# Adaptive sums moved from TensorE to VectorE, and the first taps of a depthwise convolution moved from VectorE to TensorE

## The reference, cut to what matters

```
silu_c = jax.nn.silu(c)
silu_cc = jax.nn.silu(c_ctx)
for i in range(DEPTH):
    mod_x = (silu_c @ ada_w[i] + ada_b[i])[:, None, :]
    mod_c = (silu_cc @ ada_w[i] + ada_b[i])[None, None, :]
    sx1, cx1, gx1, sx2, cx2, gx2 = jnp.split(mod_x, 6, axis=-1)
    sc1, cc1, gc1, sc2, cc2, gc2 = jnp.split(mod_c, 6, axis=-1)
```

```
z = h @ pw1_w + pw1_b
a, g = jnp.split(z, 2, axis=-1)
u = a * jax.nn.sigmoid(g)
u = dwconv(u, dw_w, dw_b)              # 31 taps, each channel by itself
u = jax.nn.silu(layernorm(u, ln_g, ln_b))
return u @ pw2_w + pw2_b
```

## Time and profile before

| | us |
|---|---|
| median of 3 runs | 1666.97 (1666.66 to 1667.65) |
| the profiled execution, its own time | 1666.32 |
| its span in the trace | 1664.5 |
| TensorE, matmuls busy | 1645.6 (99%) |
| VectorE busy | 956.1 (57%) |
| ScalarE busy | 675.9 (41%) |
| GpSimd busy | 174.3 (10%) |
| mean granted TensorE clock | 0.998 of full speed |

### The profile page before, as it was taken

How to read it: one execution, slowest core, us unless ns; L and a number is a source line. 1 busy time by engine, 2 the same in 40 slices (tenths; PEclk the granted TensorE clock), 3 DMA queues, 4 the chain that set the end, 5 groups by cost and what they waited for, 6 DMA issues and landing times.

```text
span 1664.5 us, 25807 instructions
## 1 busy us (share of the span) xinstructions
PE 1645.6 (99%) x10126; PEld 1437.0 (86%) x10126; DVE 956.1 (57%) x1498; ACT 675.9 (41%) x1015; POOL 174.3 (10%) x190
## 2 busy tenths in 40 slices
PE   8999989999999999999999999999999999999998
PEld 6777758998888888888899999999999888888888
DVE  6999987753433332234358665756566754543445
ACT  4656667632323222223354433324145533332334
POOL 1488841000000000000000000000000000000001
PEclk9999999999999999999999999999999999999999
DMA  9666642121222112212113120212112223232321
GB/s 384 233 236 246 252 190 79 62 86 38 73 70 72 54 63 65 67 59 69 45 52 94 63 76 33 83 51 70 57 59 78 97 88 117 89 100 89 101 88 52
DMA packets 40729, 165.74 MB, mean 100 GB/s; under 512 B 5089, under 2 KB 6369, under 8 KB 34497
## 3 DMA queue, kind: packets, MB, share of 16 engines
q1 hardware_dynamic: 38384, 151.55, 26.5%
q0 software_dynamic: 2256, 12.98, 2.2%
HBM read 162.41 MB, written 2.10 MB: 99 GB/s over the span
## 4 chain that ended last, share of the span: by engine, by line
PE 78%; DVE 5%; ACT 2%; issue 0%; DVEq 0%; ACTq 0%
PE ps L663 78%; DVE rstd L1637 1%; DVE H_lo L1672 1%; DVE w_lo L1631 1%; DVE tmp L1660 1%; DVE sq L1660 0%; DVE rstd L1648 0%; ACT sq L1230 0%; DVE X L1995 0%; ACT tmp L1230 0%; ACT H_hi L1221 0%; DVE H_lo L1670 0%; ACT tmp L1358 0%; DVE conv L2108 0%; PE ps L1076 0%
## 5 line engine op out<-in xcount | busy, mean ns | idle before, releaser
L663 PE MATMUL ps<-H_hi,w_hi 128*128 128x512 f32 (+1 forms) x1712 | 582.9, 340 | 4.0 <-DVE H_lo L1670 2.7
L663 PE MATMUL ps<-H_lo,w_hi 128*128 128x512 f32 (+1 forms) x1712 | 578.4, 338 | 0.0
L663 PE MATMUL ps<-H_hi,w_lo 128*128 128x512 f32 (+1 forms) x1712 | 577.9, 338 | 0.0
L663 PEld LDWEIGHTS ps<-H_hi,w_hi 128*128 128x128 f32 x1712 | 324.6, 190 | 57.2 <-issue 19.1
L663 PEld LDWEIGHTS ps<-H_hi,w_lo 128*128 128x128 f32 x1712 | 324.5, 190 | 35.1
L663 PEld LDWEIGHTS ps<-H_lo,w_hi 128*128 128x128 f32 x1712 | 324.8, 190 | 34.4
L1631 DVE TENSOR_TENSOR w_lo<-w_raw,w_hi 128x1024 fp32r<-128x1024 f32 x208 | 255.2, 1239 | 107.8 <-ACT w_hi L1183 74.8
L663 PE MATMUL ps<-mid_hi,w_hi 128*128 128x512 f32 (+1 forms) x592 | 199.4, 337 | 0.5
L663 PE MATMUL ps<-mid_lo,w_hi 128*128 128x512 f32 (+1 forms) x592 | 198.1, 335 | 0.0
L663 PE MATMUL ps<-mid_hi,w_lo 128*128 128x512 f32 (+1 forms) x592 | 198.1, 335 | 0.0
L2139 DVE SCALAR_TENSOR_TENSOR tmp<-ps,par,tmp 128x511 f32<-128x511 f32 x66 | 41.6, 657 | 231.3 <-ACT tmp L1516 155.0
(11 more groups left out here) (277 smaller groups left out, 2109.6 us busy)
## 6 DMA issues: line engine op xcount, KB each, us to landing
w_raw<-in_w_units SPq DMA_DIRECT2D x190, 512.0 KB, 3.5
ada<-in_ada_groups SPq DMA_DIRECT2D x38, 1024.0 KB, 6.4
w_raw<-in_w_units SPq DMA_DIRECT2D x16, 384.0 KB, 3.3
ada<-in_ada_groups POOLq DMA_DIRECT2D x4, 1024.0 KB, 10.5
ada_more<-in_ada_groups POOLq DMA_DIRECT2D x4, 1024.0 KB, 13.3
X<-in_x_cols SPq DMA_DIRECT2D x4, 768.0 KB, 7.5
w_raw<-in_w_units POOLq DMA_DIRECT2D x2, 512.0 KB, 14.2
ada_half<-in_ada_groups POOLq DMA_DIRECT2D x1, 1024.0 KB, 19.3
```

Source lines behind the costliest of these rows:

```text
L663: return nc.tensor.matmul(o, a, b, start=first, stop=last, skip_group_check=True)
```

## The change

Two things are changed.

**1. The second layer's adaptive sums leave TensorE.** The 12 groups of layer 1 are no longer loaded, multiplied or transposed. Layer 0 keeps its 12. Instead, the matrix of layer 1 comes transposed as 48 tiles of 128 output channels x 1024 inputs (`ada_cols`). After the norm ahead of the first FFN, GpSimd loads SiLU's two input vectors, spread to all partitions (`c_rows`), and then these tiles, 512 KB each, into two buffers (`mod_tile`). In the first FFN VectorE multiplies a tile with the vector and sums along the row in one instruction: 64 jobs, 32 for the 16 tiles that both streams need and 32 for the latents alone. They stand behind each pair from the second on, three in a slot and four in the last. A buffer is loaded again once its job is done (`mod_job`). VectorE's loop over the pairs is written out. Before the last output phase both ScalarE and VectorE wait until layer 1's modulation is made (`mod_ready`, 16).

**2. Two or four of the sum taps go to TensorE.** In blocks 0, 2, 4, 6 the first two sum taps, in blocks 1, 3, 5 the first four are matmuls with diagonal matrices (`first_sums`), amid the gate unit of the next block, after its second or third of eight input tiles. ScalarE makes the diagonals (`sum_diagonals`), and adds the bias to the sum in PSUM; VectorE goes on from there. Both weight splits of a block move to its start on ScalarE and VectorE.

```
+PE_SUM = [2, 4]
+MOD_TILES = 48
+MOD_BUFS = 2
+MOD_JOBS = [(j, v) for j in range(2 * KT) for v in range(2)] + [(j, 0) for j in range(2 * KT, MOD_TILES)]
+MOD_SLOTS = FT - 1
...
@ gpsimd
+            pool.wait_ge(h_lo_ready, KT * PARTS_BEFORE[3])
+            for v in range(2):
+                pool.dma_start(silu_rows[v], c_rows[v:v + 1, :].to_broadcast([P, D])).then_inc(c_rows_in, 16)
+            for n, (j, _) in enumerate(MOD_JOBS):
+                if n >= MOD_BUFS:
+                    pool.wait_ge(mod_job, n - MOD_BUFS + 1)
+                pool.dma_start(mod_tile[:, n % MOD_BUFS, :], ada_cols[j]).then_inc(mod_tile_in[n % MOD_BUFS], 16)
...
@ tensor
+            def first_sums(n, made, b):
+
+                pe.wait_ge(sum_diag_ready, made)
+                pe.wait_ge(both_ready, b + 1)
+                for j in range(n):
+                    m = mm(sum_acc, sum_diag[:, j, :], both_phases[:, j:j + HALF], j == 0, j == n - 1)
+                m.then_inc(sum_seeded, 1)
...
+                    pe.wait_ge(sig_ready, b)
+                    streams = [(slot(0, 1), LATS), (ps[:, 5, 0:CTX], CTXS)]
+                    unit, steps = 4 * i + 2 * q, 2 if q else 3
+                    unit_product(unit, 2 * q, KT, (H_hi, H_lo), streams, None, None, 0, steps)
+                    first_sums(PE_SUM[1 - q], 6 * i + (2 if q else 0), 2 * i + (q - 1))
+                    unit_product(unit, 2 * q, KT, (H_hi, H_lo), streams, k0=steps)
+                    pe.wait_ge(slot_read[0], b + S_PW1 // 2)
+                    unit_product(unit + 1, 2 * q + 1, KT, (H_hi, H_lo),
+                                 [(slot(0, 0), LATS), (ps[:, 2, 0:CTX], CTXS)], first_done=value_lat_done)
+                    if q:
+                        ada_transposes(i + 4)
+                    else:
+                        ada_products(i + 4)
...
@ scalar
+                split_hi(2 * b + 4, (2 * b + 4) % RING)
+                split_hi(2 * b + 5, (2 * b + 5) % RING)
                 act.wait_ge(slot_read[0], S_PW1 // 2 + b + 1)
                 if b >= 2:
                     act.wait_ge(conv_ready, b - 1)
-                products(b, range(0, 6))
-                ada_copy(2 * b + 5)
-                split_hi(2 * b + 4, (2 * b + 4) % RING)
-                products(b, range(6, 11))
+                products(b, range(0, 4))
+                if b and b % 2 == 0:
+                    ada_copy(b // 2 + 4)
...
+                if b < KT - 1:
+                    act.wait_ge(sum_seeded, b + 1)
+                    A(sum_acc, sum_acc, ACT.Identity, bias=sum_w[:, ODD_TAPS * KT + b:ODD_TAPS * KT + b + 1]) \
+                        .then_inc(sum_biased, 1)
+                products(b, range(4, 11))
...
@ vector, the loop over blocks
-                taps(b, range(0, LEAD))
-                ada_sum(4 + 2 * b, 0, 4 + b)
-                taps(b, range(LEAD, 6))
-                split_lo(2 * b + 4, (2 * b + 4) % RING)
...
+                for u in (2 * b + 4, 2 * b + 5):
+                    split_lo(u, u % RING)
+                even_tap(b, 0)
+                if b % 2:
+                    ada_sum((b - 1) // 2 + 4, 0, (b - 1) // 2 + 4)
+                even_tap(b, 1)
+                n = PE_SUM[b % 2]
+                for j in range(n, EVEN_TAPS):
+                    sum_tap(b, j)
+                    if j - n + 2 < DVE_EVEN:
+                        even_tap(b, j - n + 2)
...
@ vector, the first FFN, behind each pair
+            def mod_jobs(slot):
+
+                for n in range(len(MOD_JOBS) * (slot - 1) // MOD_SLOTS, len(MOD_JOBS) * slot // MOD_SLOTS):
+                    j, c = MOD_JOBS[n]
+                    buf = mod_tile[:, n % MOD_BUFS, :]
+                    dve.wait_ge(silu_rows_ready, 2)
+                    dve.wait_ge(mod_tile_in[n % MOD_BUFS], 16 * (n // MOD_BUFS + 1))
+                    v.tensor_tensor_reduce(buf, buf, silu_rows[c], 1.0, 0.0, ALU.mult, ALU.add,
+                                           accum_out=mod[:, 1, j, c:c + 1]).then_inc(mod_job, 1)
...
+                        modulation(len(MOD_JOBS), 1, 0, 48, 13)
+                        dve.wait_ge(mod_ready, 16)
                         out_phase_norm(blk, s, x_at, both, 3 + 2 * layer)
```

215 lines of the change are left out of this document (113 added, 102 removed).

## The result

| | before | changed |
|---|---|---|
| median (lowest to highest), us | 1667.31 (1666.66 to 1668.09), 4 runs | 1676.29 (1673.48 to 1679.12), 4 runs |
| ratio to before, 95% interval | | 1.0054 [1.0036, 1.0071] |
| mean granted TensorE clock of the runs | 0.998 in the profiled one | 0.995, 0.994, 0.993, 0.992 from the fastest to the slowest |
| profiled execution, its span | 1666.32, 1664.5 | 1673.48, 1671.7 |

The account below looks back on a forecast made before the run. VectorE, slower than TensorE by half a microsecond, was taken to bound the convolution loop, TensorE the whole; -9.9 us in the loop and +2.0 in the last slot gave -7.9, 1659.1 us, range 1654 to 1667.

Parts of the forecast that it names:

- loop, blocks 0 to 7: Convolution loop: VectorE saves 12.0 us and gives back 2.1, so 9.9 us shorter, 20.6 us a block.
- norm and second pointwise product: Stage behind the loop: TensorE's part is hidden behind ScalarE and VectorE; taken as 0, between -0.5 and +0.5 us.
- first FFN's pairs and three output phases: First FFN: VectorE's slot with jobs takes 15.5 us against 16.61 for a pair, so 20 slots cost nothing.
- last slot: End of first FFN: the output phase waits for the last four jobs and modulation; 2.0 us, between 0 and 5.
- VectorE's saving in the loop: Blocks 1 to 6: fewer sum taps and reductions, 1.52 us in even and 2.47 in odd blocks, together 12.0 us.
- the price of the block's start: Loop: VectorE's two splits at the block's start partly meet GpSimd's adds; 0.35 us more a block, 2.1 over six.
- The pair: VectorE's two weight splits at a block's start: 0.7 us less to 0.9 us more than now, 0.35 more taken.
- That GpSimd has 21.29 us of work: Rival, loop: GpSimd becomes the bound at 21.29 us a block, gaining only 5.9 us; 1663 us, chance 0.18.
- They start when the convolution's last row is made and move as a whole: The 49.14 us of norm and second pointwise product behind the loop, on chains through ScalarE and VectorE, keep their length.
- the jobs: First FFN: 64 VectorE jobs of 1.22 us each fit in the slots; pairs stay 16.6 us apart.
- the hand-over: Loop: VectorE's wait for TensorE's seeded sum and ScalarE's bias costs nothing, 1.4 us of cover; the rival's chance 0.17.
- "DVE blocks DMA" trap: First FFN: if jobs delayed GpSimd's loads by 1.2 us, a slot of 16.7 us, still covered; 1660 to 1661 us.

Follow-up runs that it names:

- e4: The change with four sum taps on TensorE in every block, where it has two in the even ones; 1672.61 us, 1.0035.
- e9: e7 with one even tap moved to VectorE from the ScalarE product and GpSimd add, leaving GpSimd 14 adds; 1668.34 us, 1.0005.
- e5: The change with the ninth adaptive group's products moved ahead of TensorE's wait for the last block's values; 1673.44 us, 1.0032.
- e1: The change with short matmuls added in TensorE's waits, 10 before seeded sums of two taps and 30 before the layer norm's mean; 1677.41 us, 1.0057.
- e10: e7 with 14 short matmuls on TensorE ahead of the tenth group's products, during its wait for the last row; 1668.25 us, 1.0002.
- e13: The change with 2 of GpSimd's 64 loads in the first FFN, jobs multiplying the two silu(c) rows with each other; 1674.00 us, 1.0049.
- e7: The change with four sum taps every block, ninth group's products earlier, jobs ending a slot earlier, last adaptive group's load ahead of a weight load; 1669.07 us, 1.0009.
- e14: The change with all 64 loads but VectorE's jobs of 32 columns in place of 1024; 1674.05 us, 1.0054.
- e3: The change with VectorE's two splits of a block put back behind sum taps 6 and 13; 1689.38 us, 1.0128.

## Why the prediction was wrong

The forecast was 1659.1 us, the range 1654 to 1667, with 0.11 for slower. In the profiled executions the terms are, forecast and measured:

| term | forecast | measured |
|---|---|---|
| loop, blocks 0 to 7 | -9.9 | -3.6 |
| last block, up to the first variance | 0 | +3.3 |
| norm and second pointwise product | 0 | +0.1 |
| first FFN's pairs and three output phases | 0 | +1.65 |
| last slot | +2.0 | +1.9 |
| end of the span | 0 | +2.7 |
| start to block 0 | 0 | +1.2 |

They add up to +7.2 us, from 1664.5 to 1671.7. The profiled run is the fastest of the four; the slowest has a span of 1677.3 and a clock of 0.992 for 0.995. A mean clock lower by 0.003 over 1677 us is 5 us of TensorE's full pace withheld, about the 5.6 us by which it is longer. That is worked out, its trace was not seen.

**VectorE's saving in the loop was right, the price of the block's start was the step that failed first.** "The pair could cost 0.7 us less than now or 0.9 us more; I take 0.35": against the same blocks before it cost nothing more in blocks 1 and 5, 0.4 in block 3 and 0.8 to 1.1 in blocks 2, 4 and 6, together 2.8 us where 2.1 were forecast. But the forecast priced the pair alone. The sum of the phases (+1.7 us over the six blocks) and the first even tap (+2.7) meet GpSimd too, and they stood in the sum at nothing. So 7.2 us of the 12.0 were given back and not 2.1; the rest of what is missing, 1 us, is spread over the blocks. I had read GpSimd's pause of 1.05 us as slack of its own against becoming the bound, and used it to argue that the splits would fall into it; a faster VectorE takes the pause away. That GpSimd has 21.29 us of work was a rival at 0.18; its time for the loop (-5.9) is what e4 came to (-6.2), but e9 leaves its mechanism 0.2 us a block at most.

**"They start when the convolution's last row is made and move as a whole" was the second.** It held from the first variance on, to 0.1 us. It did not hold for the last block, for which I had listed no cost. The change counts one set of products fewer in the stage behind, and I costed TensorE's part there at nothing "as the stage hangs on ScalarE and VectorE"; but that set had come to stand in a chain of TensorE with 0.31 us to spare. By e5 its place is worth 1.7 us of the 3.3; by the rows, 1.4 us are the four mean matmuls at the low clock. The other 1.5 us are VectorE's own delay in that block: the sum of the phases and the first even tap, 0.4 us each, and 0.68 us of waiting for the even row, for which ScalarE's two splits now stand in the way. That last is read from rows, no run moved these splits alone.

**The clock was not in the forecast at all.** Taking 28 us of work off TensorE and giving back 13 left holes of 1.4 to 4.8 us, and behind the two longest the clock stood at the low level. Nothing in the earlier trace rows, with clock 1.00, warned of it, but that TensorE would wait was in my text ("by under 2 us" for `both_phases`, 2.82 at the longest), and I priced the wait only. In the loop it was free (e1), behind it it was not (e5, e10), and between the FFNs it made 501.3 to 501.5 us of 499.9 in three of the variants with the last slot's wait.

**The last slot, the jobs, the hand-over were right.** 1.93 us of wait against 2.0, pairs at 16.7 us, jobs of 1.22 us, VectorE waiting once for the seeded sum, by 0.2 us. The jobs as a case of the Trainium skill's box on the "DVE blocks DMA" trap (SBUF — State Buffer) came to nothing: loads land in 3.9 us in the median, near the 3.5 of SyncE's. The forecast's slot of 16.7 us for that case was called covered, which against 16.61 it was not.

**The end of the span was a term that I did not have**: 2.2 of the 2.7 us by GpSimd's loads or its program for them (e13). Open are the 0.55 us in each output phase, which neither loads, nor the length of the jobs, nor the written-out program, nor semaphores make, each tried by itself. The 1.2 us at the start may be chance: block 0's product comes at 53.1 to 54.4 us in three kernels without the change and at 53.0 to 56.1 in thirteen with it or a part of it.

With its costs repaired (e7, e9, e10) the change is level with the kernel before, 1.0002 to 1.0009. No version was faster than it.

## What to carry to other kernels

When work comes off an engine that was never idle, ask what its neighbour's idle moment was for: a pause of GpSimd between two blocks was what made VectorE's start of block cheap, and it vanished ahead of every block that followed a shortened one. Nor do repairs simply add up: once one has moved the bound, another may only lengthen a wait, and lower the clock behind it, as the moved products did in e7. Follow every moved step to the place where it now stands, a step taken off one chain stands in another; and where TensorE will wait longer than before, price the low clock of the microseconds behind the wait along with it. Count the end of the program too: 62 more loads, long landed, came with 2.2 us there.

## What was not expected of the hardware

- 62 loads of 512 KB on GpSimd's queue, all landed 840 us before, put the end of the span 3.0 us behind the last bytes, where it is 0.8 us with two of them or none; GpSimd's longer program for them was not tried apart.
- After a wait of 2.82 us TensorE's next window had 0.57 of its clock; after 1.69 and 1.42 us at similar places, and after 2.84 us at the same place in e14, it had 1.00. The wait of 1.9 us in the last slot left it at 1.00 in the change and at 0.57 to 0.61 in e1, e3 and e4, so the length of a wait alone does not tell.
- VectorE and GpSimd held each other up on both sides: a 1024-column split 1.9 us for 1.22, GpSimd's add of 393 columns 1.4 to 1.9 us for 0.9 to 1.0.
